# A flow-matching backbone step on one core: two projection chunks per norm tile, and another order of the PSUM pairs

## The chip, the cores and the metric

One core of a Trainium2 chip runs the kernel. The metric is device time in microseconds (us), the median of several executions. The engines are PE (TensorE, matmuls), ACT (ScalarE), DVE (VectorE), POOL (GpSimd) and SP (SyncE, which here only issues the weight DMAs). They run side by side and wait for each other through semaphores only.

## The reference, cut to what matters

The model has two layers. Each one norms its 640 tokens (128 context, 512 latent) and multiplies them with one wide input matrix; everything else in the layer hangs on that product.

```python
D_MODEL = 1024; DEPTH = 2; SEQ = 128; DEC_SEQ = 512
...
def trunk_layer(x, cond, p, rope, ctx_k, ctx_v):
    mod = (jax.nn.silu(cond) @ p['mod_w'] + p['mod_b']).reshape(-1, 1, 6 * D)
    sh1, sc1, g1, sh2, sc2, g2 = jnp.split(mod, 6, axis=-1)
    h = rms_norm(x, p['norm1_w']) * (1 + sc1) + sh1
    proj = h @ p['w_in']
    hy, qkv, scv, gates = jnp.split(proj, [HY_COLS, HY_COLS + ATT_COLS, HY_COLS + ATT_COLS + SC_COLS], axis=-1)
    ya = hyena_mixer(hy, ...)     # starts with a 3-tap convolution over the tokens
    ...                           # attention, short convolution, gates, merge, experts
```

## The kernel before, in words

**Layout.** Activations lie feature-major: `X` is 128 partitions x 8 tiles of features (KC = 8) x 640 tokens. Weights come as a stream of 1 MB items into the four slots of `ring`; SP issues the load of an item when `item_used` says that the last user of its slot is done (L419).

**Precision.** A product of fp32 operands is made of three fast passes. Weights and activations are each split into a high and a low part, and high x high, high x low and low x high are added (`passes`). ACT copies the high part of a half item (128 output features) to `W2` (`split`, L1008), DVE subtracts it to get the low part (L1348). `W2` has two places, so the split of half item u waits for the end of the chunk that used u - 2.

**A chunk** (`chunk`, L557) is 128 output features for all tokens: 8 feature tiles x 3 passes x 2 halves of 320 tokens = 48 matmuls of 128x320, each with its own weight load, accumulated in a pair of PSUM banks. The pairs are numbered 0 (banks 0, 1), 1 (banks 2, 3) and 2 (banks 4, 5); chunk c of the first 24 uses pair c % 3. Its last matmul raises `chunk_ready`. Banks 6 and 7 take transposes.

**The norm** at the head of a layer. PE makes the mean squares (L570), ACT the root (L1034), DVE the reciprocal, and PE spreads it over the partitions into pair 1 (L575). Then, feature tile by feature tile, DVE multiplies X by it (L1371, in two pieces: 128 and 512 tokens), ACT adds the shift and rounds to the high part (L1039), and DVE makes the low part (L1360) and raises `x_lo`, once a tile. DVE runs one tile ahead: L1371 of tile k + 1, then L1360 of tile k.

**The first chunks.** PE's loop over c = 0 to 23 is written out in program order: wait for the split half item c (`half_ready`, which for odd c also raises `item_used`), for c of 3 or more wait for the pair to be free, then the chunk; behind chunks 1 to 8 come the transposes of the chunk before it (`transposes(c - 1)`, L682, five of 128x128). Chunk 0 alone waits for `x_lo` before each feature tile. Chunk 1 runs after it without waits inside.

**What a chunk sets off.** For c below 12, ACT waits for chunk c, copies it from PSUM to `raw` in two pieces (L1008, 128x128 and 128x512), then splits half item c + 2. DVE splits half item c + 2 too and then makes the 3-tap convolution of `raw` into `cv` (`conv`: L1508 and two times L1511, 128x641), and raises `conv_done`. `transposes(c)` waits for that. All queues are in order.

Of the kernel before, what the change touches and what calls it, by code (L numbers as in the profile page):

```python
# [28 lines left out]
KC = D // P  # L29
DEPTH = 2  # L30
LI, LS = 128, 512
T = LI + LS
# [3 lines left out]
HALVES = ((0, T // 2), (T // 2, T))  # L36
# [66 lines left out]
def build(nc, a):  # L103
    with ExitStack() as ctx:
# [43 lines left out]
        ps = ctx.enter_context(nc.psum_tensor("ps", [P, 8, 512], F32))  # L148
# [36 lines left out]
        Y3 = region(56, [3, 4, T])  # L185
        u_tm, x1_tm = region(86, [NT, DH]), region(96, [NT, DH])
        qkv = region(106, [NT, QKV])
        raw, cv = region(121, [2, T + 3]), region(126.25, [2, T + 1])
        ubuf = region(131.5, [2, T])
# [61 lines left out]
        x_hi, x_lo = sem("operand_hi"), sem("operand_lo")  # L251
        OP_Y, OP_M, OP = KC, KC + 12, KC + 12 + KC
        w_hi, w_lo = sem("weights_hi"), sem("weights_lo")
        chunk_ready = sem("chunk_ready")
        act_freed, dve_freed = sem("act_freed"), sem("dve_freed")
# [68 lines left out]
        def tokh(b):  # L324

            return ps[:, 2 * b:2 * b + 2, :].rearrange("p a n -> p (a n)")[:, 192:832]

        def w2(u, kc, part):

            return W2[:, u % 2, part, :].rearrange("p (k n) -> p k n", k=kc)  # L330
# [208 lines left out]
        def _(pe):  # L539
# [11 lines left out]
            def chunk(b, w, src, n, wait=None):  # L551

                for k, wp, hp, first, last in passes(n):
                    if wait and wp + hp == 0:
                        wait(k)
                    for c0, c1 in HALVES:
                        mm = pe.matmul(tokh(b)[:, c0:c1], w(wp)[:, k, :], src(hp, k)[:, c0:c1], start=first, stop=last)  # L557
                return mm
# [109 lines left out]
            for l in range(DEPTH):  # L668
# [13 lines left out]
                        mm = pe.transpose(ps[:, 6 + t // 4, P * (t % 4):P * (t % 4) + P], cv[:, c % 2, cols], ident[:])  # L682
                    mm.then_inc(tr_ready, 1)

                for c in range(24):
                    half_ready(l, c)
                    if c >= 3:
                        wait_chunk_freed(pe, l, c - 3)

                    wait = (lambda k: pe.wait_ge(x_lo, l * OP + k + 1)) if c == 0 else None  # L690
                    chunk(c % 3, lambda part: w2(c, KC, part), h_part, KC, wait).then_inc(chunk_ready, 1)
                    if 1 <= c <= 8:
                        transposes(c - 1)
                for i in range(3):

                    for hf in range(2):
                        half_ready(l, 24 + 2 * i + hf)
                        for u in range(3):
                            n = 24 + 3 * i + u
                            if hf == 0:  # L700
                                wait_chunk_freed(pe, l, n - 3)
                            for t in range(2 * u, min(2 * u + 2, NT)):
                                for k, wp, hp, first, last in passes(4):
                                    mm = pe.matmul(ps[:, 2 * (n % 3) + t % 2, 0:256],  # L704
                                                   h_part(hp, 4 * hf + k)[:, P * t:P * t + P],
                                                   w2(hf, 4, wp)[:, k, :], start=first and hf == 0, stop=last and hf == 1)
                            if hf or u == 2:
                                mm.then_inc(chunk_ready, 1)
# [15 lines left out]
                for t in range(NT):  # L724
                    if t >= 2:
                        pe.wait_ge(a_trev, l * 6 + t - 1)
                    for j in range(4):
                        mm = pe.transpose(ps[:, t % 2, P * j:P * j + P], qkv[:, t, P * j:P * j + P], ident[:])
                    mm.then_inc(a_tr, 1)
                for t in range(NT):  # L730
                    mm = pe.transpose(ps[:, 2 + (t + 3) // 4, P * ((t + 3) % 4):P * ((t + 3) % 4) + P],
                                      qkv[:, t, NQ * HD:QK], ident[:])
# [48 lines left out]
                for j in range(4):  # L781
                    for g in range(2):
                        mm = pe.matmul(ps[:, 4 + g, P * j:P * j + P], qT[head(g), j, 0:P], kT[head(g), 0:P],
                                       start=True, stop=True)
# [3 lines left out]
                for g in range(2):  # L788
                    for j in range(4):
                        mm = pe.transpose(ps[:, 4 + g, P * j:P * j + P], Pp[:, g, P * j:P * j + P], ident[:])  # L790
# [3 lines left out]
                for g in range(2):  # L794
                    mm = pe.matmul(ps[head(g), 6, :], qkv[:, 0, QK + HD * g:QK + HD * g + HD], PTp[:, g, :],
                                   start=True, stop=True)
# [13 lines left out]
                for o in range(2):  # L810
# [35 lines left out]
                    for r in range(2):  # L846
                        mm = pe.matmul(ps[:, 4 + r, :], csi[:, r, :], u_tm[:, 0, :], start=True, stop=True)
# [4 lines left out]
                    if o == 0:  # L852
                        for r in range(2):
                            mm = pe.matmul(ps[:, 6, :], csi[:, r, :], Yp[:, r, :], start=r == 0, stop=r == 1)
                    else:
                        for m in range(4):
                            for r in range(2):
                                mm = pe.matmul(ps[:, 6, P * m:P * m + P], Yp[:, r, P * m:P * m + P], csi[:, r, :],
                                               start=r == 0, stop=r == 1)
# [35 lines left out]
                for n in range(2 * NT):  # L895
                    t, hf = n // 2, n % 2
# [109 lines left out]
        def _(act):  # L1006
            def copy(o, i):
                return act.activation(o, i, ACT.Copy)  # L1008
# [101 lines left out]
            for l in range(DEPTH):  # L1110
# [13 lines left out]
                for c in range(24):  # L1124
                    if 2 <= c <= 9:
                        evac_tr(c - 2)
                    if freed_by(c)[0] == "act":
                        wait_chunk(act, l, c)
                        if c < 12:
                            if c >= 2:  # L1130

                                act.wait_ge(conv_done, l * 12 + c - 1)
                            copy(raw[:, c % 2, 1:1 + LI], tokh(c % 3)[:, 0:LI])
                            copy(raw[:, c % 2, 2 + LI:2 + T], tokh(c % 3)[:, LI:T]).then_inc(act_freed, 1)
                        else:
                            if c >= 18:
                                act.wait_ge(dve_freed, l * 8 + c % 2 + 1)
                            copy(ubuf[:, c % 2, :], tokh(c % 3)).then_inc(act_freed, 1)
                    split(l, c + 2)
                for n in range(9):  # L1140
                    i, u = n // 3, n % 3
                    if u == 0:

                        split(l, 26 + 2 * i)
                    wait_chunk(act, l, 24 + n)
                    t1 = min(2 * u + 2, NT)
                    b = 2 * ((24 + n) % 3)
                    copy(qkv[:, 2 * u:t1, 256 * i:256 * i + 256], ps[:, b:b + t1 - 2 * u, 0:256]).then_inc(act_freed, 1)
                    if u == 2:
                        split(l, 27 + 2 * i)  # L1150
# [190 lines left out]
        def _(dve):  # L1341
# [152 lines left out]
            for l in range(DEPTH):  # L1494
# [20 lines left out]
                for c in range(24):  # L1515
                    b = c % 2
                    settle()
                    split(l, c + 2)
                    if c < 12:
                        before = (c // 2) * 2 + c % 2  # L1520
                        dve.wait_ge(act_freed, l * A_FREED + before + 1)
                        if 2 <= c < 8 or c in (8, 9):
                            dve.wait_ge(tr_ready, l * 8 + c - 1)
                        ins = conv(cv[:, b, :], lambda i: raw[:, b, i:i + T + 1], V_HYW + 3 * c, V_HYB + c)
                        if c < 8:
                            ins.then_inc(conv_done, 1)
                        else:
                            settle()
                            dve.tensor_copy(Y3[:, 0, c - 8, 0:LI], cv[:, b, 0:LI])
                            dve.tensor_copy(Y3[:, 0, c - 8, LI:T], cv[:, b, LI + 1:T + 1]).then_inc(conv_done, 1)  # L1530
                        continue
                    if freed_by(c)[0] == "act":
                        continue
                    j = 2 * ((c - 12) // 6) + b
                    settle()
                    wait_chunk(dve, l, c)
                    pieces = ((0, LI, 0), (LI, T, 1))
                    if (c - 12) % 6 < 4:

                        dve.wait_ge(act_freed, l * A_FREED + freed_by(12 + 6 * ((c - 12) // 6) + b)[1])  # L1540
                        for c0, c1, x in pieces:
                            ins = dve.tensor_tensor(raw[:, b, 1 + c0 + x:1 + c1 + x], tokh(c % 3)[:, c0:c1],
                                                    ubuf[:, b, c0:c1], ALU.mult)
                        ins.then_inc(dve_freed, 1)
                        settle()
                        conv(cv[:, b, :], lambda i: raw[:, b, i:i + T + 1], V_SCW + 3 * j, V_SCB + j)
                    else:
                        for c0, c1, x in pieces:
                            ins = dve.tensor_tensor(Y3[:, 2, j, c0:c1], tokh(c % 3)[:, c0:c1],
                                                    cv[:, b, c0 + x:c1 + x], ALU.mult)  # L1550
                        ins.then_inc(dve_freed, 1)

# [404 lines left out]
```

## Time and profile before

| | |
|---|---|
| Median of 3 runs | 2566.1 us (2566.07 to 2567.58) |
| The profiled execution | 2564.07 us |
| Its span | 2562.4 us |
| PE busy | 2286.4 us (89%) |
| DVE, ACT, POOL busy | 1122.7, 739.0, 162.5 us |
| Granted PE clock, mean of the span | 0.938 |
| PE's share of the chain that ended last | 82% |

The profile is of one execution. The chain that ended last is followed back from the last instruction, at each step to what released it; an engine's share of it tells how much of the end hangs on that engine. The granted clock is a share of PE's full speed: 1.0 is 2.4 GHz, 0.5 is 1.2 GHz. Layer 0 begins at about 260 us of the span and layer 1 at about 1410 us; before layer 0 lies a prologue.

### The profile page before, as it was taken

The page shows a single profiled execution, that of the slowest core. Times are in us where ns is not written, and L with a number is a line of the kernel's source. Part 1 is how long each engine was busy: PE and PEld are TensorE (multiplying, and loading weights), DVE is VectorE, ACT ScalarE, POOL GpSimd, SP SyncE. Part 2 cuts the span into 40 slices and gives each one's busy share as a digit, 9 for nine tenths or more (in the row PEclk, how much of TensorE's full clock was granted, in tenths as well). Part 3 has the DMA queues.
Part 4 walks back from the last instruction along what each step waited for, and adds up shares of the span by engine and source line. Part 5 has one row for each costly group of instructions (what it writes and reads, how often), then busy time and mean ns, then how long its engine had stood idle before and what let it go on. Part 6 is the DMA issues. An engine that isn't in the chain of part 4 may idle for free.

```text
span 2562.4 us, 35187 instructions
## 1 busy us (share of the span) xinstructions
PE 2286.4 (89%) x13744; PEld 1840.1 (72%) x13744; DVE 1122.7 (44%) x1778; ACT 739.0 (29%) x1302; POOL 162.5 (6%) x218
## 2 busy tenths in 40 slices
PE   4999899999797998599996899999787998699995
PEld 2444799999663996466664899999654996466664
DVE  2454544341358654333334544331368654333333
ACT  1332321222350223133332321222350323233332
POOL 0001000000100100011110000000100100011100
PEclk8599899999998998799998899999898998799998
DMA  8687112133401431899993122233401421899992
GB/s 304 230 317 282 64 67 83 72 132 113 172 1 41 141 114 60 296 350 346 344 341 119 56 77 72 77 128 123 161 1 41 155 101 75 292 355 345 341 330 93
DMA packets 71938, 436.28 MB, mean 170 GB/s; under 512 B 9225, under 2 KB 9737, under 8 KB 30794
## 3 DMA queue, kind: packets, MB, share of 16 engines
q1 hardware_dynamic: 45216, 329.27, 35.3%
q0 software_dynamic: 21872, 89.44, 11.4%
q10 hardware_dynamic: 4732, 15.93, 1.7%
q8 instruction: 82, 1.34, 0.2%
q14 instruction: 36, 0.29, 0.0%
HBM read 384.46 MB, written 50.15 MB: 170 GB/s over the span
## 4 chain that ended last, share of the span: by engine, by line
PE 82%; DVE 7%; DMA 4%; ACT 3%; issue 2%; DVEq 1%; ACTq 0%; POOLq 0%; POOL 0%
PE ps L557 36%; PE ps L939 17%; PE ps L962 7%; PE ps L704 3%; PE ps L639 2%; PE ps L591 2%; PE ps L621 2%; DMA back<-in_cft 1%; PE ps L747 1%; PE ps L836 1%; PE ps L833 1%; PE ps L599 1%; PE ps L819 1%; PE ps L892 1%; ACT front L1008 1%
## 5 line engine op out<-in xcount | busy, mean ns | idle before, releaser
L557 PE MATMUL ps<-front_r 128*128 128x320 f32 x5888 | 935.0, 312 | 25.0 <-DVE front_r L1360 10.4
L557 PEld LDWEIGHTS ps<-front_r 128*128 128x128 f32 x5888 | 886.3, 190 | 31.4 <-issue 10.3
L1348 DVE TENSOR_TENSOR front_r<-ring,front_r 128x1024 fp32r<-128x1024 f32 x148 | 181.0, 1224 | 465.8 <-ACT front_r L1008 464.7
L1008 ACT ACTIVATE front_r<-ring 128x1024 fp32r<-128x1024 f32 x148 | 156.0, 1055 | 395.7 <-PE ps L557 292.9
L1008 ACT ACTIVATE back<-ps 128x480 f32<-128x480 f32 (+4 forms) x236 | 111.3, 496 | 438.3 <-PE ps L557 165.9
L939 PE MATMUL ps<-ring,back 128*80 128x256 f32 x1024 | 231.5, 386 | 1.9 <-ACT back L1008 1.9
L939 PEld LDWEIGHTS ps<-ring,back 128*80 128x80 f32 x1024 | 154.9, 153 | 70.4 <-issue 6.6
L962 PE MATMUL ps<-back_r,front_r 128*80 128x512 f32 x768 | 198.8, 404 | 0.0
L939 PE MATMUL ps<-front,back 128*80 128x256 f32 x768 | 168.3, 379 | 0.0
L939 PEld LDWEIGHTS ps<-front,back 128*80 128x80 f32 x768 | 115.1, 150 | 51.0
L557 PE MATMUL ps<-back_r,front_r 128*128 128x320 f32 x640 | 148.4, 314 | 0.0
L962 PEld LDWEIGHTS ps<-back_r,front_r 128*80 128x80 f32 x768 | 109.0, 148 | 52.0
L1775 DVE TENSOR_TENSOR back<-ps,back 80x256 f32<-80x256 f32 x64 | 26.9, 421 | 260.7 <-PE ps L939 260.7
L557 PEld LDWEIGHTS ps<-back_r,front_r 128*128 128x128 f32 x640 | 109.4, 192 | 0.0
L1292 ACT ACTIVATE back<-ps 80x256 f32<-80x256 f32 x64 | 24.3, 379 | 294.4 <-PE ps L939 294.4
L1158 ACT ACTIVATE back<-ps 128x640 f32<-128x640 f32 x48 | 33.8, 705 | 229.1 <-PE ps L557 229.1
L1008 ACT ACTIVATE front<-ps 128x512 f32<-128x512 f32 (+3 forms) x126 | 62.7, 564 | 113.6 <-PE ps L819 83.2
L591 PE MATMUL ps<-ring,cs 128*32 128x256 f32 x768 | 67.8, 483 | 22.4 <-ACT back L1008 11.3
L704 PE MATMUL ps<-front_r 128*128 128x256 f32 x720 | 86.7, 283 | 0.0
L704 PEld LDWEIGHTS ps<-front_r 128*128 128x128 f32 x720 | 86.6, 192 | 0.0
L528 POOL DMA_INDIRECT acc<-back,idx x32 | 45.8, 1432 | 595.9 <-issue 559.5
L1787 DVE TENSOR_TENSOR back_r<-front,back_r 128x512 fp32r<-128x512 f32 x128 | 81.1, 684 | 3.2 <-ACT back_r L1008 3.1
(208 smaller groups left out, 2431.3 us busy)
## 6 DMA issues: line engine op xcount, KB each, us to landing
ring<-in_stream SPq DMA_DIRECT2D x186, 1024.0 KB, 5.9
front<-in_stream SPq DMA_DIRECT2D x80, 1024.0 KB, 8.6
back<-in_stream SPq DMA_DIRECT2D x48, 1024.0 KB, 7.5
gates<-back POOLq DMA_DIRECT2D x48, 320.0 KB, 2.4
back<-gates POOLq DMA_DIRECT2D x48, 320.0 KB, 3.3
kspec<-back POOLq DMA_DIRECT2D x20, 512.0 KB, 6.7
back<-kspec POOLq DMA_DIRECT2D x4, 2560.0 KB, 11.9
rows<-front ACTq DMA_DIRECT2D x10, 520.0 KB, 2.7
```

The costliest lines, as they stand in the source:

```text
L528: pool.indirect_dma_start(a[f"acc{l}"], bass.IndirectOffsetOnAxis(ap=idx[:, e:e + 1], axis=0), yo[:, e % 2, :], None, compute_op=ALU.add). ...
L557: mm = pe.matmul(tokh(b)[:, c0:c1], w(wp)[:, k, :], src(hp, k)[:, c0:c1], start=first, stop=last)
L591: mm = pe.matmul(ps[32 * j:32 * j + 32, 6, 0:256], cs[:, k, :], w[:, k, :], start=k < 4, stop=k >= 4)
L621: mm = pe.matmul(ps[:, 4 + d, :], fh2[l][:, P * t:P * t + P], w3[:, l, w0:w0 + DH], start=True, stop=True)
L639: mm = pe.matmul(ps[:, b + odd, :], cft[:, r, 2 * odd + t, P * kt:P * kt + P], (fa, fb)[r][:, unit % 2, 1 + 2 * odd + t, :], start=t == 0, ...
L704: mm = pe.matmul(ps[:, 2 * (n % 3) + t % 2, 0:256], h_part(hp, 4 * hf + k)[:, P * t:P * t + P], w2(hf, 4, wp)[:, k, :], start=first and hf ...
L939: mm = pe.matmul(ps[0:SLOTS, 2 * hf + which, 0:256], x[:, k, :], w[:, k, :], start=k == 0, stop=k == KC - 1)
L962: mm = pe.matmul(ps[0:SLOTS, 6 + c, :], hidT[hp][:, ee % 2, k, :], W4[:, v % 4, wp, :], start=k + n == 0, stop=k == 3 and n == 2)
L1008: return act.activation(o, i, ACT.Copy)
L1158: act.activation(sgb[:, n % 2, :], tokh(n % 4), ACT.Sigmoid).then_inc(sg_ready, 1)
L1348: dve.tensor_tensor(half_dst(u, 1), src, half_dst(u, 0).bitcast(F32), ALU.subtract).then_inc(w_lo, 1)
L1787: dve.tensor_tensor(W4[:, v % 4, 1, :], quarter_item(l, ee, v)[1], W4[:, v % 4, 0, :].bitcast(F32), ALU.subtract).then_inc(e_wlo, 1)
```

## The change

The first two chunks of each layer are worked together. PE waits for both half items at the start, then for each feature tile of the norm it issues the six matmuls of chunk 0 and the six of chunk 1, pass by pass in turn. `chunk_ready` is raised by chunk 0's last matmul and by chunk 1's. The loop goes on with `transposes(0)` and chunk 2. The pairs of banks are used in the order 0, 2, 1, since pair 1 holds the spread root until the norm's last tile; every place that names a pair for the first 33 chunks goes through `third`.

```diff
+        def third(c):
+            return (0, 2, 1)[c % 3]
...
+                half_ready(l, 0)
+                half_ready(l, 1)
+                for k, wp, hp, first, last in passes(KC):
+                    if wp + hp == 0:
+                        pe.wait_ge(x_lo, l * OP + k + 1)
+                    for c in range(2):
+                        for c0, c1 in HALVES:
+                            mm = pe.matmul(tokh(third(c))[:, c0:c1], w2(c, KC, wp)[:, k, :], h_part(hp, k)[:, c0:c1],
+                                           start=first, stop=last)
+                        if last:
+                            mm.then_inc(chunk_ready, 1)
-                for c in range(24):
+                for c in range(1, 24):
+                    if c == 1:
+                        transposes(0)
+                        continue
                     half_ready(l, c)
                     if c >= 3:
                         wait_chunk_freed(pe, l, c - 3)
-                    wait = (lambda k: pe.wait_ge(x_lo, l * OP + k + 1)) if c == 0 else None
-                    chunk(c % 3, lambda part: w2(c, KC, part), h_part, KC, wait).then_inc(chunk_ready, 1)
+                    chunk(third(c), lambda part: w2(c, KC, part), h_part, KC).then_inc(chunk_ready, 1)
                     if 1 <= c <= 8:
                         transposes(c - 1)
```

The readers of the pairs on ACT and DVE change `c % 3` to `third(c)` in the same way, and nothing else; these two engines, POOL and SP issue the same instructions in the same order as before.

PE's order around the head of layer 0, of the kernel before, from the norm's sixth tile to chunk 3 (`front_r` holds the split weights and activations, `operand_lo` is the semaphore `x_lo`, `weights_lo` is `w_lo`; line 557 is `chunk`, line 682 the transposes):

```order
L557 MATMUL ps<-front_r 128x320 [waits operand_lo]
L557 MATMUL ps<-front_r 128x320 x5
L557 MATMUL ps<-front_r 128x320 [waits operand_lo]
L557 MATMUL ps<-front_r 128x320 x5
L557 MATMUL ps<-front_r 128x320 [waits weights_lo]
L557 MATMUL ps<-front_r 128x320 x47
L682 MATMUL ps<-ident,back 128x128 [waits conv_done]
L682 MATMUL ps<-ident,back 128x128 x4
L557 MATMUL ps<-front_r 128x320 [waits weights_lo]
L557 MATMUL ps<-front_r 128x320 x47
```

The same place of PE in the changed kernel (line 697 is the new loop, 561 is `chunk`, 686 the transposes):

```order
L697 MATMUL ps<-front_r 128x320 [waits operand_lo]
L697 MATMUL ps<-front_r 128x320 x11
L697 MATMUL ps<-front_r 128x320 [waits operand_lo]
L697 MATMUL ps<-front_r 128x320 x11
L686 MATMUL ps<-ident,back 128x128 [waits conv_done]
L686 MATMUL ps<-ident,back 128x128 x4
L561 MATMUL ps<-front_r 128x320 [waits weights_lo]
L561 MATMUL ps<-front_r 128x320 x47
```

The 48 matmuls that stood between the last feature tile and the transposes of chunk 0 now stand ahead of that tile's end, six with each of the eight tiles; the transposes, with their wait on `conv_done`, follow the norm's last tile directly.

## Rows read from the trace of the kernel before

**Rows 1.** The page: engines over the span, and the chain that ended last

```profile
PE 2286.4 (89%) x13744; PEld 1840.1 (72%) x13744; DVE 1122.7 (44%) x1778; ACT 739.0 (29%) x1302; POOL 162.5 (6%) x218
PE 82%; DVE 7%; DMA 4%; ACT 3%; issue 2%; DVEq 1%; ACTq 0%; POOLq 0%; POOL 0%
```

**Rows 2.** The chain, head of layer 0: start us, us, what

```profile
267.87 1.02 DVE front L1371 x2
...
281.10 0.94 DVE front_r L1360 x2
...
282.07 1.14 PE ps L557 x6
...
283.25 8.19 PE ps L557 x54
291.43 0.59 PE ps L682 x5
292.02 7.04 PE ps L557 x48
```

**Rows 3.** The chain, head of layer 1

```profile
1432.50 8.18 PE ps L557 x54
```

**Rows 4.** Timeline of layer 0: start us, us, engine line op, tiles, count [idle before <-releaser]

```profile
271.12 6.58 PE L557 MATMUL ps<-front_r 128*128 128x320 f32 x24 [3.29 <-DVE front_r L1360]
272.87 1.57 PEld L557 LDWEIGHTS ps<-front_r 128*128 128x128 f32 x6 [0.21 <-DVE front_r L1360]
...
283.24 7.92 PEld L557 LDWEIGHTS ps<-front_r 128*128 128x128 f32 x54 [0.29 <-DVE front_r L1360]
283.34 29.34 SPq L419 DMA_DIRECT2D ring<-in_stream  x3
284.49 0.77 ACT L1008 ACTIVATE back<-ps 128x128 f32<-128x128 f32 x2 [2.35 <-PE ps L557]
...
286.23 1.23 DVE L1348 TENSOR_TENSOR front_r<-ring,front_r 128x1024 fp32r<-128x1024 f32 x1 [3.04 <-ACT front_r L1008]
...
288.06 1.85 DVE L1511 SCALAR_TENSOR_TENSOR back<-back,vec 128x641 f32<-128x641 f32 x2
```

**Rows 5.** Windows: busy of PE, PEld, DVE, ACT, POOL, then granted clock, DMA, GB/s

```profile
270.00:276.00 6.00, 4.88 (x17) 4.43 (x18) 6.00 (x14) 3.27 (x8) 0.00 (x0) 0.50 0.01 3
276.00:277.00 1.00, 0.99 (x6) 0.73 (x6) 1.00 (x3) 0.62 (x2) 0.00 (x0) 0.88 0.00 0
1426.00:1427.00 1.00, 1.00 (x6) 1.00 (x6) 1.00 (x4) 0.30 (x1) 0.00 (x0) 0.73 0.00 0
684.00:686.00 2.00, 0.00 (x0) 0.00 (x0) 1.85 (x3) 0.63 (x2) 0.00 (x0) 0.96 1.04 422
686.00:689.00 3.00, 2.79 (x10) 2.08 (x12) 1.41 (x5) 0.78 (x1) 0.00 (x0) 0.50 1.02 418
689.00:690.00 1.00, 1.00 (x10) 0.51 (x8) 0.00 (x0) 0.24 (x1) 0.00 (x0) 0.87 1.04 426
675.00:676.00 1.00, 1.00 (x6) 0.64 (x5) 0.00 (x0) 0.65 (x2) 1.00 (x2) 0.70 0.13 33
935.00:938.00 3.00, 3.00 (x14) 3.00 (x13) 2.79 (x4) 0.30 (x1) 0.00 (x0) 0.50 0.00 0
938.00:940.00 2.00, 2.00 (x14) 2.00 (x13) 0.00 (x0) 0.00 (x0) 0.00 (x0) 0.89 0.00 0
```

**Rows 6.** Timeline of PE: restarts after idle stretches, and 128x320 matmuls at either clock

```profile
672.53 4.23 PE L728 MATMUL ps<-ident,back 128*128 128x128 f32 x20 [7.72 <-POOLq L294]
686.21 1.97 PE L790 MATMUL ps<-ident,front 128*128 128x128 f32 x8 [5.71 <-DVE front L1637]
933.58 0.56 PE L557 MATMUL ps<-front_r 128*128 128x320 f32 x2 [1.89 <-DVE back L1712]
935.24 1.27 PE L557 MATMUL ps<-front_r 128*128 128x320 f32 x4
936.31 0.73 PE L557 MATMUL ps<-back_r,front_r 128*128 128x320 f32 x2
```

More of the change, by code:

```diff
@@ L703, in _ @@
                                 for k, wp, hp, first, last in passes(4):
-                                    mm = pe.matmul(ps[:, 2 * (n % 3) + t % 2, 0:256],
+                                    mm = pe.matmul(ps[:, 2 * third(n) + t % 2, 0:256],
                                                    h_part(hp, 4 * hf + k)[:, P * t:P * t + P],
@@ L1132, in _ @@
                                 act.wait_ge(conv_done, l * 12 + c - 1)
-                            copy(raw[:, c % 2, 1:1 + LI], tokh(c % 3)[:, 0:LI])
-                            copy(raw[:, c % 2, 2 + LI:2 + T], tokh(c % 3)[:, LI:T]).then_inc(act_freed, 1)
+                            copy(raw[:, c % 2, 1:1 + LI], tokh(third(c))[:, 0:LI])
+                            copy(raw[:, c % 2, 2 + LI:2 + T], tokh(third(c))[:, LI:T]).then_inc(act_freed, 1)
                         else:
@@ L1137, in _ @@
                                 act.wait_ge(dve_freed, l * 8 + c % 2 + 1)
-                            copy(ubuf[:, c % 2, :], tokh(c % 3)).then_inc(act_freed, 1)
+                            copy(ubuf[:, c % 2, :], tokh(third(c))).then_inc(act_freed, 1)
                     split(l, c + 2)
@@ L1146, in _ @@
                     t1 = min(2 * u + 2, NT)
-                    b = 2 * ((24 + n) % 3)
+                    b = 2 * third(24 + n)
                     copy(qkv[:, 2 * u:t1, 256 * i:256 * i + 256], ps[:, b:b + t1 - 2 * u, 0:256]).then_inc(act_freed, 1)
@@ L1541, in _ @@
                         for c0, c1, x in pieces:
-                            ins = dve.tensor_tensor(raw[:, b, 1 + c0 + x:1 + c1 + x], tokh(c % 3)[:, c0:c1],
+                            ins = dve.tensor_tensor(raw[:, b, 1 + c0 + x:1 + c1 + x], tokh(third(c))[:, c0:c1],
                                                     ubuf[:, b, c0:c1], ALU.mult)
@@ L1548, in _ @@
                         for c0, c1, x in pieces:
-                            ins = dve.tensor_tensor(Y3[:, 2, j, c0:c1], tokh(c % 3)[:, c0:c1],
+                            ins = dve.tensor_tensor(Y3[:, 2, j, c0:c1], tokh(third(c))[:, c0:c1],
                                                     cv[:, b, c0 + x:c1 + x], ALU.mult)
```

## The prediction

> **What bounds the kernel now.** I read the page first: PE is busy for 89% of the span and carries 82% of the chain that ended last [rows 1]. So a stage is worth what it adds to or takes from PE's path. The chain then shows the place of the change [rows 2]. From 267.87 to 282.03 us it runs through DVE alone: L1371 and L1360 in turn, 0.92 to 1.02 us each, so a feature tile comes about every 1.84 us: PE takes up the second at 272.87 and the seventh at 282.07 [rows 2, 4]. PE waits for each. From 283.25 the chain is PE without a break: the last tile of chunk 0 (6 matmuls) and chunk 1 (48) in 8.19 us, the transposes in 0.59, chunk 2 in 7.04, which is 0.147 us a matmul. Layer 1 has the same step, 54 matmuls in 8.18 us [rows 3]. The reader should see that chunk 1 does two jobs: it fills PE, and it covers the way from chunk 0's end to the convolution that `transposes(0)` waits for.
>
> I count from S, the start of PE's first matmul on a tile: 271.12 [rows 4]. Chunk 2 starts at 292.02, so at S + 20.90, in layer 0. That is the figure to beat.
>
> **What the change takes away.** Chunk 1's own 7.04 us behind the norm are gone, in each layer. The number of matmuls and weight loads is the same.
>
> **What the joint tiles take.** In the first tiles PE has the 1.2 GHz clock. It shows 0.50 in 270 to 276 and 0.88 in 276 to 277, so it rises at 276.24, 5.1 us after S; in layer 1 0.73 in 1426 to 1427 puts the rise at 1426.54, 6.2 us after that layer's first tile at 1420.4 (1432.50 less the 12.1 us from 271.12 to 283.25) [rows 3 to 5]. At that clock four matmuls of 128x320 take 1.07 us (935.24 to 936.31), 0.267 each [rows 6]. Six take 1.6 us, which just fits a tile's 1.84; twelve take 3.2 and do not. So PE falls behind DVE as long as the clock is low. At the full clock twelve take 1.76 us, no more than a tile's cadence, so PE doesn't catch up either: the joint stretch is bound by PE, not DVE. With a low stretch of x us it ends at S + x + (96 - x / 0.267) x 0.147. For x I take 4.2 us, the mean of the time spent working at the low clock at five restarts that I can read: 5.1 and 6.2 here, 3.1 from 672.53 (the 0.70 in 675 to 676 puts the rise at 675.6), 3.1 from 686.21 (the 0.87 in 689 to 690 puts it at 689.3) and 3.4 from 935.0, behind the restart at 933.58 (0.89 in 938 to 940: 938.4) [rows 5, 6]. That gives 16 matmuls at 0.267 and 80 at 0.147: **the joint stretch ends at S + 16.0** (15.5 with 3.1 us, 16.9 with 6.2). Before, chunk 1 ended at 291.43, S + 20.3. So 4.3 us are won, not 7.04.
>
> **What the change adds: a wait.** `transposes(0)` now follows at once and waits for `conv_done`. The way to it hangs on chunk 0's end, which now lies two matmuls before the joint end. Before, chunk 0's last matmul started at about 283.98 (the sixth at 0.147 from 283.24) and ACT took up the copy at 284.49, 0.51 later. The convolution ended at 288.06 + 1.85 = 289.91 [rows 4]. So 5.42 us lie between ACT's start and its end: two copies, ACT's split, DVE's split of 1.23 and three convolution steps, all in series, with both engines idle before them (2.35 and 3.04 us). None of it starts sooner now. Chunk 0's last matmul starts 0.44 before the joint end, so ACT starts 0.07 after it, and the transposes can start at 0.07 + 5.42 + 0.05 (DVE's end to PE's start, as the 0.03 from 281.10 + 0.94 to 282.07 [rows 2]) = **5.54 us after the joint end**. In that time PE has nothing: chunk 2 stands behind the transposes, though its weights are split 3.0 us after the joint end (287.46 against 284.49). Before, the convolution was done 1.5 us before PE came to it, so the cover was there, with little to spare.
>
> **What the wait does to the clock.** An idle stretch of 5.71 us before 686.21 left the clock at 0.96 in 684 to 686 and at 0.50 from 686 on; even one of 1.89 us before 933.58 was followed by a low stretch, 935 to 938.4 [rows 5, 6]. So after 5.5 us idle I take the low clock for granted. Work went on at it for 3.1 to 6.2 us in the five cases above, 4.2 in the mean, and half of that is lost: **2.1 us** (1.55 to 3.1). The transposes are in it (20 take 4.23 us at the low clock [rows 6], so five take 1.06 in place of 0.59). They matter in one more way. In [rows 5] the clock rose at 675.6 while the engine had done nothing but the transposes of L728. I go by that: the five transposes count as work from their first. The Trainium skill, in TensorE: Matmul & The Clock Gate, Part 4 on the PE-mode transpose, says that the full clock does not engage for transposes, as they do not count as busy in the same way. By that rule the return would be counted only from chunk 2, 1.06 us later, which costs 0.5 us more in each layer and makes the total below 2573.8; the trace speaks against it.
>
> **Sum for a layer.** 16.0 + 5.54 + 0.59 (transposes) + 2.1 = S + 24.2, against S + 20.9: **3.3 us later**. From chunk 2 on the cadence is as before: chunk 3 needs the split that DVE makes right behind the first convolution, 1.23 us, and transposes(1) its convolution 2.5 us later, both within chunk 2's 7.04. The delay is not absorbed, since PE carries the chain to the layer's end.
>
> **Costed at nothing.** The order of the banks: the same number of PSUM accesses, and the halves of one chunk already alternate between two banks at 0.147 us. Waiting for both half items at the start: both are split before the root is spread. The load of a weight item: `item_used` for the first item is raised some 18 us sooner, so SP's DMA moves from 283.34 [rows 4] to the norm; at its old place DVE's split beside it took 1.23 us, as long as later ones, and PE waits for no load in this stage.
>
> **Total.** Two layers: +6.7 us (twice 3.33). On the profiled execution's own 2564.07 us that is 2570.8; its time lies 2.0 us under the median, so against the median of 2566.1 it gives **2572.8 us**. About 0.2%, 5.1 us, is what a measurement of this kernel can tell from no change.
>
> **Rivals.**
> *The clock holds through the wait.* Then 2.1 us a layer fall away and a layer loses 16.0 + 5.54 + 0.59 - 20.9 = 1.2 us, 2.5 in all: 2568.6 us, no measurable change. Against it stand 684 to 689 and 935 to 938 in [rows 5]; for it only that a drop may come late.
> *Not slower: PE keeps pace with the norm.* If the denser work brought the clock up with the first tile, the joint stretch would be bound by DVE. It would end 12 matmuls after the last tile, which came at 283.24 (S + 12.1): S + 13.9. With the clock also held, chunk 2 starts at S + 20.0, 0.9 us sooner, 1.8 us in all: 2564.3 us. It decides from a joint stretch of under 14.8 us. Against it: in layer 1 the clock rose only 6.2 us after S [rows 5], though six matmuls a tile keep PE at work 1.6 us of 1.84 at that clock.
> *Interleaving four banks slows the matmuls,* or a chunk behind waits as well. At 0.02 us a matmul it is 2 us a layer more: 2576.7 us. Nothing in the trace shows such a price.
> *The change doesn't do what it says:* if DVE's tiles slowed beside twice the matmuls, the stretch would be bound by DVE after all; since PE sets it with 2 us to spare, this costs nothing until a tile takes over 2.1 us.
>
> **How the numbers follow.** My forecast has 0.83, of it 0.75 slower by over 5.1 us and 0.08 under that, since its bounds are 15.5 + 5.54 + 0.59 + 1.55 - 20.9 = 2.3 us and 16.9 + 5.54 + 0.59 + 3.1 - 20.9 = 5.2 us a layer, 4.6 and 10.4 in all. The clock that holds has 0.07, the pace kept 0.05 (0.02 of it in a gain over 0.2%, from what I don't see), slower matmuls 0.05. That makes 0.80 slower, 0.18 the same, 0.02 faster. The range takes in the held clock below (2568.6) and the upper bound (2576.5): 2568.5 to 2577.
>
> **What would show it.** In the changed profile: joint matmuls without a gap from the second tile on, ending about 16 us after the first; then PE idle for 5.5 us, released by DVE's L1511 step (its convolution) in both layers; then a granted clock of 0.5 for some 3 to 6 us; chunk 2 starting 3 us later than now, counted from the first tile. I am wrong if that idle stretch is under 4 us, if the clock stays at 1.0 behind it, or if the joint stretch ends before S + 15.

## The result, and the profile after

The changed kernel takes 2574.38 us (median of 8 runs, 2572.67 to 2575.86) against 2566.8 us before (8 runs, 2566.07 to 2567.86). The ratio is 1.0028 with a 95% interval of 1.0017 to 1.0039: slower by 7.6 us in the medians, 4.4 to 10.0 by the interval. The forecast was 2572.8 us, slower. It was added up on the median of 2566.1 us that stood on record for the kernel before; its own difference was 6.7 us, against the 7.6 measured.

The engines' busy times are nearly as before (PE 2288.7 us against 2286.4 in [rows 1]). The time went where PE has nothing to do, and into the clock behind it. Below is the chain of waits of the changed kernel at the head of layer 0, to be laid beside [rows 2]. Each line has its start in us, its length in us, and what ran. Line 697 is the joint loop, 561 `chunk`, 686 the transposes, 1026 ACT's copies, 1366 DVE's split, 1378 DVE's low part of an activation tile, 1529 the convolution:

```profile
272.18 1.02 DVE front_r L1378 x2
273.21 0.04 issue
273.25 16.78 PE ps L697 x94
...
290.12 0.07 ACT back L1026
...
290.77 1.07 ACT front_r L1026
291.83 0.02 issue
291.86 1.23 DVE front_r L1366
...
294.64 0.90 DVE back L1529
295.55 0.04 issue
295.59 1.33 PE ps L686 x5
296.92 8.39 PE ps L561 x48
305.30 0.59 PE ps L686 x5
305.89 7.04 PE ps L561 x48
```

Three things are to be seen. The steps of DVE for seven more tiles, which [rows 2] had, are gone: the chain is on PE from the first tile on, 94 matmuls without a gap (the 94th is chunk 0's last). Then it leaves PE for ACT and DVE, at 290.03, and comes back at 295.59; before, it never left PE there. And the first transposes and chunk 2 are longer, 1.33 and 8.39 us in place of 0.59 and 7.04. Layer 1 shows the same, with a longer chunk 2:

```profile
1426.46 15.46 PE ps L697 x94
...
1447.47 1.33 PE ps L686 x5
1448.80 9.19 PE ps L561 x48
1457.99 0.59 PE ps L686 x5
```

The timeline names in brackets how long the engine was idle before a line, and what released it; first two lines of layer 0, then one of layer 1:

```profile
273.25 17.06 PE L697 MATMUL ps<-front_r 128*128 128x320 f32 x96 [3.19 <-DVE front_r L1378]
295.59 1.33 PE L686 MATMUL ps<-ident,back 128*128 128x128 f32 x5 [5.28 <-DVE back L1529]
1447.47 1.33 PE L686 MATMUL ps<-ident,back 128*128 128x128 f32 x5 [5.28 <-DVE back L1529]
```

And the windows, with the columns of [rows 5], give the granted clock, third from the end:

```profile
279.00:280.00 1.00, 1.00 (x7) 1.00 (x7) 1.00 (x3) 0.33 (x2) 0.00 (x0) 0.85 0.00 0
280.00:292.00 12.00, 10.31 (x71) 10.05 (x69) 5.41 (x12) 4.61 (x11) 0.00 (x0) 1.00 0.01 1
292.00:293.00 1.00, 0.00 (x0) 0.00 (x0) 1.00 (x2) 1.00 (x2) 0.00 (x0) 0.97 0.00 0
293.00:299.00 6.00, 3.41 (x14) 3.41 (x15) 5.61 (x8) 1.12 (x2) 0.00 (x0) 0.50 0.00 0
299.00:300.00 1.00, 1.00 (x6) 1.00 (x5) 0.30 (x1) 0.00 (x0) 0.00 (x0) 0.61 0.00 0
1429.00:1430.00 1.00, 1.00 (x6) 1.00 (x6) 1.00 (x3) 0.80 (x2) 0.00 (x0) 0.71 0.00 0
1446.00:1447.00 1.00, 0.00 (x0) 0.00 (x0) 0.93 (x2) 0.00 (x0) 0.00 (x0) 0.82 0.00 0
1453.00:1454.00 1.00, 1.00 (x7) 1.00 (x6) 0.00 (x0) 0.00 (x0) 0.00 (x0) 0.76 0.00 0
```

A window's mean clock between 0.5 and 1.0 tells when it changed: 0.85 over one microsecond is 0.3 us at half speed and 0.7 us at full speed. So the 2.4 GHz level came at 279.3, went at 292.9 in the middle of the idle stretch, and was back at 299.8, 4.2 us after PE took up work. In layer 1 it came at 1429.6, went at 1446.6 and was back at 1453.5, 6.0 us after PE's restart at 1447.47.

Counted from PE's first matmul on a tile, chunk 2 ended 305.30 - 273.25 = 32.05 us later in layer 0 and 31.53 in layer 1; before it was 299.06 - 271.12 = 27.94 in both (chunk 2's end is 292.02 + 7.04 in [rows 2]). That is +4.11 and +3.59, 7.7 us together, which agrees with the measured loss of 7.6. The two spans differ by 10.6 us; 2.1 of the other 2.9 lie ahead of layer 0 (first tile at 273.25 against 271.12), where both kernels have the same instructions. Across all profiles of this study that first tile lay anywhere between 271.0 and 273.25, so it is no part of the change.

### The profile page after: what moved, and what is told of

It reads as the page before. It is cut to its first block, busy times and chain, and to the rows that moved or that the text cites. A ratio compares the mean times of both kernels' runs of the same rounds, so it can differ in the third digit from the quotient of the medians.

```text
span 2573.0 us, 35185 instructions
## 1 busy us (share of the span) xinstructions
PE 2288.7 (89%) x13744; PEld 1844.1 (72%) x13744; DVE 1123.0 (44%) x1778; ACT 739.0 (29%) x1302; POOL 162.8 (6%) x218
## 4 chain that ended last, share of the span: by engine, by line
PE 82%; DVE 7%; DMA 4%; ACT 3%; issue 2%; DVEq 1%; ACTq 0%; POOLq 0%; POOL 0%
PE ps L561 35%; PE ps L957 17%; PE ps L980 7%; PE ps L722 3%; PE ps L595 2%; PE ps L643 2%; PE ps L625 2%; DMA back<-in_cft 1%; PE ps L765 1%; PE ps L697 1%; PE ps L854 1%; PE ps L851 1%; PE ps L837 1%; PE ps L603 1%; PE ps L910 1%
## 5 line engine op out<-in xcount | busy, mean ns | idle before, releaser
L561 PE MATMUL ps<-front_r 128*128 128x320 f32 x5696 | 902.1, 311 | 14.6 <-DVE back_r L1710 8.2
L561 PEld LDWEIGHTS ps<-front_r 128*128 128x128 f32 x5696 | 857.5, 190 | 16.8 <-DVE front_r L1366 8.9
L1026 ACT ACTIVATE front_r<-ring 128x1024 fp32r<-128x1024 f32 x148 | 156.0, 1055 | 395.9 <-PE ps L561 292.9
L722 PEld LDWEIGHTS ps<-front_r 128*128 128x128 f32 x720 | 86.6, 192 | 0.0
```

The source lines that it names most:

```text
L722: mm = pe.matmul(ps[:, 2 * third(n) + t % 2, 0:256], h_part(hp, 4 * hf + k)[:, P * t:P * t + P], w2(hf, 4, wp)[:, k, :], start=first and h ...
```

## The experiments

Theory A is the forecast's: the loss is PE's wait for the first convolution, plus the low clock behind it. Theory B puts it on the PSUM side: other banks, or more of them in turn, make the matmuls dearer. Each run stands beside runs of the kernel before on the same chip, whose medians were 2566.38 (runs 1, 2, 4, 5), 2566.27 (runs 3, 7, 8, 9) and 2565.83 us (runs 6, 10). The ratios are against these. Where a run is set against the changed kernel's 2574.38, that one stood beside a kernel before of 2566.8; counted from the kernel before on either side, such a gain is 0.4 to 1.0 us smaller.

**1. The order of the banks alone.**

```diff
-                half_ready(l, 0)
-                half_ready(l, 1)
-                for k, wp, hp, first, last in passes(KC):
...
-                for c in range(1, 24):
-                    if c == 1:
-                        transposes(0)
-                        continue
+                for c in range(24):
...
-                    chunk(third(c), lambda part: w2(c, KC, part), h_part, KC).then_inc(chunk_ready, 1)
+                    wait = (lambda k: pe.wait_ge(x_lo, l * OP + k + 1)) if c == 0 else None
+                    chunk(third(c), lambda part: w2(c, KC, part), h_part, KC, wait).then_inc(chunk_ready, 1)
```

> Only the order of the PSUM pairs (0, 2, 1) is taken from the change; chunks 0 and 1 run one after the other as before. Theory A (the loss is the wait of the transposes on the first convolution, plus the low clock behind it): no difference from before, 2566.8 us within 1 us, and chunk 2 starts 20.9 us after PE's first matmul on a tile. Theory B (other banks or more of them in turn make PE's accesses dearer): part of the 7.6 us shows here, at least 2 us.

Measured: 2566.0 us, ratio 1.0 (0.9991 to 1.0009). Its chain has the steps of [rows 2] to a hundredth:

```profile
284.01 8.18 PE ps L561 x54
292.19 0.59 PE ps L686 x5
292.77 7.04 PE ps L561 x48
```

The order of the banks is free, within the 2.3 us to either side that the interval leaves, and by the chain to a hundredth. It is what permits the joint chunks, not what they cost.

**2. A shorter wait: the split of half item 2 in place of the convolution.** On the changed kernel:

```diff
-                for c in range(1, 24):
-                    if c == 1:
-                        transposes(0)
-                        continue
+                for c in range(2, 24):
...
-                    if 1 <= c <= 8:
-                        transposes(c - 1)
+                    if 2 <= c <= 9:
+                        transposes(c - 2)
```

> The changed kernel with every group of transposes one chunk later: chunk 2 comes straight behind the joint chunks, then the transposes of chunk 0, chunk 3, the transposes of chunk 1 and so on. Theory A: PE now waits only for DVE's split of half item 2, 3.0 us after the joint end in place of 5.5, so 2.5 us a layer are won back; the clock still falls, a little less often. 5 to 6 us less than the changed kernel's 2574.4, so 2568 to 2569.5 us. Theory B: nothing is won by it, 2574 us.

Measured: 2567.55 us, ratio 1.0003 (0.9994 to 1.0012); 6.8 us less than the changed kernel, half a microsecond under what was expected. The timeline:

```profile
290.95 8.62 PE L561 MATMUL ps<-front_r 128*128 128x320 f32 x48 [2.83 <-DVE front_r L1363]
1439.19 8.83 PE L561 MATMUL ps<-front_r 128*128 128x320 f32 x48 [2.83 <-DVE front_r L1363]
```

PE now waits 2.83 us for line 1363, DVE's split, and 48 matmuls still take 8.62 and 8.83 us where the timeline has 7.3 for them at the full clock. So 2.45 us of wait are gone in each layer; the clock costs 1.3 and 1.5 in place of 2.1 and 2.9.

**3. The control: the later transposes on the kernel before.** The same last two lines, on the kernel before.

> The kernel before with every group of transposes one chunk later and nothing else. Theory A: before the change no wait of PE stood there, so the later transposes win nothing by themselves: 2566.4 us within 1 us. If the later transposes were a gain of their own, under 2564 us, what the second run won would not be the shorter wait.

Measured: 2566.07 us, ratio 0.9998 (0.9989 to 1.0007). The later transposes gain nothing where nobody waits for them; what run 2 won is the shorter wait, and the shorter low clock behind it.

**4. The wait filled with idle matmuls.** On the changed kernel, behind the joint loop:

```diff
+                for n in range(34):
+                    c0, c1 = HALVES[n % 2]
+                    pe.matmul(tokh(1)[:, c0:c1], h_hi[:, 0, 0:P], h_hi[:, 0, 0:T // 2], start=True, stop=True)
```

> The changed kernel with 34 idle matmuls of 128x320 behind the joint chunks (operands from the high activations, output to pair 1, which chunk 2 overwrites), 5.0 us of work in a wait of 5.5. Theory A: chunk 2 starts at the same place, but the granted clock stays at 1.0 through the wait and the 2.1 us (layer 0) and 2.9 us (layer 1) that the transposes and chunk 2 lost at the low clock are back: 2574.4 - 5.0 = 2569.4 us. If the clock had no part in it: 2574.4 us or more.

Measured: 2567.61 us, ratio 1.0006 (0.9997 to 1.0015). The chain of layer 0:

```profile
272.47 16.08 PE ps L697 x94
...
294.12 0.81 PE ps L686 x5
294.92 7.04 PE ps L561 x48
```

The window over the wait:

```profile
288.00:296.00 8.00, 7.70 (x54) 7.44 (x53) 5.30 (x7) 4.02 (x7) 0.00 (x0) 1.00 0.00 0
```

The transposes still wait for the convolution (294.12, which is 21.65 us after the first tile, within what the changed kernel's two layers show: 22.34 and 21.01). But the clock stays at 1.00 and chunk 2 takes 7.04. In this profile chunk 2 ends 29.49 us after the first tile, 1.55 more than before; in layer 1 it is 1.1 more. That is the forecast's rival of the held clock, 1.2 us a layer, made real. The run won 6.8 us, or 6.4 counted from the kernel before on either side, where 5.0 were expected; the difference lies within the interval, whose half width is 2.3 us. The clock's part of the loss is thereby shown by itself: by the trace 5.0 of 7.7 us, with 2.65 left.

**5. More cover: chunk 1 three tiles behind chunk 0.**

```diff
+                def tile(c, k):
+                    if c == 0:
+                        pe.wait_ge(x_lo, l * OP + k + 1)
+                    for wp, hp in ((0, 0), (0, 1), (1, 0)):
...
+                for k in range(KC + 3):
+                    if k < KC:
+                        tile(0, k)
+                    if k >= 3:
+                        tile(1, k - 3)
```

> Chunk 1 works three feature tiles behind chunk 0 in place of beside it, so chunk 0 takes the last tile as soon as it is there and four tiles of chunk 1, 24 matmuls or 3.5 us, are left to cover the way to the first convolution. Transposes stay where the change has them. Theory A: chunk 0 ends about 13.0 us after PE's first tile, chunk 1 at 16.5, the convolution at 18.8: PE waits 2.3 us in place of 5.5, and chunk 2 starts 19.4 us plus a clock loss of 0 to 2 us after the first tile, against 20.9 before and 22.2 plus 2.5 in the changed kernel: 2563 to 2567 us. Theory B (the alternation between two chunks costs): no better than 2573 us.

Measured: 2566.73 us, ratio 1.0002 (0.9993 to 1.0011): 7.6 us less than the changed kernel, but at the upper end of what was expected.

```profile
291.84 1.33 PE L686 MATMUL ps<-ident,back 128*128 128x128 f32 x5 [2.06 <-DVE back L1534]
1441.05 0.80 PE L686 MATMUL ps<-ident,back 128*128 128x128 f32 x5 [2.06 <-DVE back L1534]
```

Those are lines of the timeline. The chain of layer 0 goes on:

```profile
291.84 1.33 PE ps L686 x5
293.17 8.04 PE ps L561 x48
```

The wait is 2.06 us, 2.3 had been worked out, but everything lies 0.7 us later: tile 7 of chunk 0 still stands behind the matmuls of chunk 1 that precede it. And even these two microseconds brought the low clock: 1.33 and 8.04 us in place of 0.59 and 7.04, so 1.7 us a layer. In layer 1 the chain has 0.80 and 8.58, 1.75 us too much, though the clock went down only 1.1 us behind the restart. Cover that is a little too short costs the wait once and the clock as well.

**6. Still more cover: six tiles behind.** `KC + 6`, `k >= 6` and `k - 6` in the loop of run 5.

> Chunk 1 six tiles behind chunk 0, the transposes where the change has them: the cover behind chunk 0's end goes from 2 matmuls (the change) past 24 (three tiles behind) to 36, 5.3 us. Theory A: chunk 0 ends 13.1 us after the first tile, chunk 1 at 18.4, the convolution is done at 18.9. PE waits about 0.5 us, the clock holds, and chunk 2 starts at 19.5 against 20.9 before: 1.4 us a layer, 2563.6 us. If a clock loss or another wait stays: 2566 us or more.

Measured: 2566.18 us, ratio 1.0001 (0.9992 to 1.001).

```profile
283.08 9.06 PE ps L697 x60
292.14 0.59 PE ps L686 x5
292.73 7.04 PE ps L561 x48
```

No wait and no low clock, as expected, but the gain of 1.4 us a layer was a slip of mine: behind chunk 0's end seven tiles of chunk 1 are left, 42 matmuls, not 36, which is 0.9 us; and ACT took up chunk 0's copy 14.06 us after the first tile, where 13.1 had been expected for chunk 0's end. Chunk 2 starts 292.73 - 272.02 = 20.7 us after the first tile, against 20.9. With so much kept for cover, nearly all of chunk 1 is behind the norm again. Runs 5 and 6 show both ends. Four or five tiles behind were not run. In run 6 the convolution ended at 291.50, 0.64 us before the transposes started, so an estimate is that less cover could win at most 0.6 us a layer more: what covers the 5.4 us to the convolution is the same work that the change wanted to move ahead.

**7. Cover and a shorter wait together.** Run 5's loop with run 2's transposes.

> Chunk 1 three tiles behind chunk 0, and the transposes one chunk later. Theory A: in the run with chunk 1 behind alone, the joint work ended 17.2 us after the first tile and DVE's split of half item 2 at about 17.0, so PE finds no wait at all and the clock stays up. Chunk 3 starts at 17.2 + 7.04 + 0.59 = 24.8 us after the first tile, against 28.3 before: 3.5 us a layer, 2559.5 us. If the split comes late by over a microsecond or the clock falls all the same: 2562 to 2564 us.

Measured: 2560.44 us, ratio 0.9977 (0.9967 to 0.9987), faster than both kernels. The chain:

```profile
276.52 11.95 PE ps L697 x78
288.47 7.04 PE ps L561 x48
295.51 0.58 PE ps L686 x5
296.10 7.04 PE ps L561 x48
```

PE goes from the joint chunks into chunk 2 without a gap and at the full clock. Chunk 3 starts 296.10 - 271.00 = 25.1 us after the first tile, against 299.65 - 271.12 = 28.5 before, 3.4 us less; in layer 1 it is 3.3. But only one group of transposes stands ahead of it here, and two stood there before, so 0.59 us of this is put off and not saved. The two kernels are level again behind chunk 9. First the kernel before, then this run:

```profile
344.82 0.59 PE ps L682 x5
```

```profile
341.86 7.04 PE ps L561 x48
348.90 0.59 PE ps L686 x5
```

Before, chunk 9 started behind these transposes, at 345.41, and took 7.04, so chunk 10 started 352.45 - 271.12 = 81.3 us after the first tile. Here chunk 9 starts at 341.86 and the transposes stand behind it; chunk 10 starts 349.49 - 271.00 = 78.5 us after the first tile, 2.8 us sooner; in layer 1 it is 2.7. The sum is 5.6, measured were 5.8. The expected 3.5 us a layer left out the same 0.59.

**8. The low clock ahead of the first tile.** On the changed kernel:

```diff
+                for n in range(12):
+                    c0, c1 = HALVES[n % 2]
+                    pe.matmul(tokh(2)[:, c0:c1], w2(0, KC, 0)[:, 0, :], W2[:, 0, 0, 0:T // 2], start=True, stop=True)
```

> The changed kernel with the same 12 idle matmuls ahead of the first tile. Theory A: the joint stretch, which PE bounds, is shorter by 0.45 of the low time that is saved, about 1.4 us a layer, and ends at or above 13.9 us after the first tile; the wait of 5.5 us and the low clock behind it stay: 2574.4 - 2.8 = 2571.6 us. If DVE's tiles bound the joint stretch: 2574.4 us.

Measured: 2569.55 us, ratio 1.001 (1.0001 to 1.0019), 4.8 us less than the changed kernel where 2.8 were expected.

```profile
272.86 14.84 PE L700 MATMUL ps<-front_r 128*128 128x320 f32 x96 [0.24 <-DVE front_r L1381]
292.98 1.33 PE L686 MATMUL ps<-ident,back 128*128 128x128 f32 x5 [5.28 <-DVE back L1532]
```

The joint stretch takes 14.84 us in place of 17.06 and 15.74, and the wait of 5.28 us is what it was. So the joint stretch is bound by PE, and its excess is the low clock. That is 3.1 us in both layers together, near the 2.8 expected. By the chain chunk 2 took 7.90 us in layer 0 and 8.10 in layer 1, in place of 8.39 and 9.19: the low clock behind the wait was also shorter in this execution, which is the other 1.6 us and nothing that the edit was meant to do. At the full clock the joint stretch ends 14.7 us after the first tile, not 13.9 as the forecast's rival had it: tile 6, the seventh, is there only at S + 10.95, and from it on 24 matmuls are to be done, 3.5 us.

**9. The same 12 idle matmuls on run 7.**

> As the run before it, with 12 idle matmuls of 128x320 between the spread of the root and the first tile, where PE waits for 3.2 us (output to pair 2, which chunk 1 overwrites). Theory A: the clock comes up about 3 us sooner, PE is less far behind when the last tile comes and the joint work ends up to 1.4 us a layer sooner: 2557 us, 2559.5 if chunk 0 was bound by DVE's tiles alone.

Measured: 2559.13 us, ratio 0.9972 (0.9961 to 0.9983), the lowest median of all, but within the interval of run 7's. Its chain has 11.96 and then 7.04 us, as run 7's; chunk 3 starts 296.74 - 271.63 = 25.1 us after the first tile, no sooner. With chunk 1 three tiles behind, PE is not late in the first tiles, so a faster clock there only lengthens its waits. By its size the outcome is the second of the two expected.

**10. The weight item given free as late as before.** On the changed kernel:

```diff
-                half_ready(l, 1)
+                pe.wait_ge(w_lo, l * UNITS + 2)
...
+                pe.sem_inc(item_used, 1)
```

> The changed kernel with one part undone: the first weight item is given free behind the joint chunks, as late as before the change, so SP's load does not fall into the norm. Theory A costs this part at nothing: 2574.4 us within 1 us. Rival: the load beside the norm slows something, and at least 1.5 us are won.

Measured: 2572.89 us, ratio 1.0026 (1.0017 to 1.0036) against the change's 1.0028. SP's load is issued behind the norm again, at 285.40 us, 13.8 us after the first tile; in the changed kernel it was at 267.70, 5.6 us ahead of it. The wait has not changed:

```profile
293.38 1.33 PE L686 MATMUL ps<-ident,back 128*128 128x128 f32 x5 [5.28 <-DVE back L1530]
```

The median is 1.5 us lower, but the kernel before was 1.0 us lower beside it; counted from that one the loss is 7.1 us in place of 7.6, and the load costs nothing that can be told.

## Why the prediction was right

**The joint stretch is bound by PE and ends at S + 16.0: right.** The records end at S + 17.06 and S + 15.74; a record runs on for 0.16 us past its matmul's turn of 0.147 (0.31 in all), so the stretch ended at S + 16.9 in layer 0 and S + 15.6 in layer 1. The spread follows the clock as the formula has it: a low stretch of 6.05 us (273.25 to 279.3) gives 16.8, one of 3.1 (1426.46 to 1429.6) gives 15.5. Run 8 is the same formula with the low stretch taken away. The forecast's 4.2 us for the low stretch was right in neither layer; 16.0 lies between the two ends, and that their mean, 16.25, comes so near it is in part luck.

**The wait: right to a tenth.** Forecast were 5.54 us from the joint end; the transposes started at 22.34 and 21.01 us, so 5.4 after it in both layers. ACT took up the copy at 290.12 and the transposes started at 295.59, 5.47 us, of which the forecast had 5.42 and 0.05. Runs 2, 5 and 6 change the wait's end or its cover, and it goes to 2.83, 2.06 and nothing.

**The clock behind it: right in kind, a little small.** 2.1 us a layer was the estimate, from restarts elsewhere in the trace. It measured (1.33 - 0.59) + (8.39 - 7.04) = 2.1 in layer 0 and 0.74 + 2.15 = 2.9 in layer 1. The forecast's reckoning that half of the low time is lost held: 2.1 us of 4.2, and 2.9 of 6.0. Against the forecast's 3.3 us a layer, layer 0 lost 0.8 more, all of it in the joint stretch (+0.9, with -0.1 from the wait); layer 1 lost 0.3 more (-0.4 in the joint stretch, -0.1 in the wait, +0.8 in the clock). Run 4 shows the clock's part by taking it away. The clock was back 4.2 and 6.0 us after the first transpose, within the 3.1 to 6.2 of the five restarts. The five transposes took 1.33 us, 0.267 each, where the forecast had 1.06: it took the mean of the 20 from 672.53, of which the last ones already ran at the full clock ([rows 5], from 675.6). The rule in the Trainium skill's TensorE: Matmul & The Clock Gate, Part 4 on the PE-mode transpose, that the full clock does not engage for transposes, could not be told from this here, as 1.33 us of them stand ahead of 8 us of matmuls; [rows 5, 6], where it rose beside transposes alone, stay the evidence against it, in the trace of before.

**What was costed at nothing.** The order of the banks (run 1), the earlier load (run 10) and the cadence from chunk 2 on (7.04 and 0.59 in the chain above) cost nothing that the runs can tell. That four banks in turn are free too follows from run 8: 96 joint matmuls in 14.7 us, where the tiles' arrival alone asks for 14.5.

**The rivals.** The held clock happened only in run 4, where it was held by work. The pace kept happened only in run 8; its bound of S + 13.9 was 0.6 us too low, since it left out that tile 6 comes only 1.17 us ahead of the last. DVE's tiles did not slow beside twice the matmuls: in layer 0 its line 1378 starts at 274.03, 275.87, 277.71 and 279.55, 1.84 us apart as before. One slip in the reading of [rows 2] changes nothing: the chain from 267.87 to 282.03 is not DVE alone, 1.02 us of it, at 268.91, are ACT's (L1039).

## What to carry to other kernels

When work is moved ahead of a wait, look first at what it covered where it stood: chunk 1 hid a chain of ACT and DVE of 5.4 us. Moving its 7.0 us ahead won only 3.4 and 4.7 us (the joint end against S + 20.3), because PE itself bound the joint stretch, and the uncovered wait and the clock behind it cost more than that. Work of two streams pass by pass makes both end at the same time, and so late; let the stream whose end sets something off lead, with enough of the other left behind it, and let the next work in the queue be what is ready first (run 7: 5.8 us under the kernel before, while each half alone, runs 2 and 5, only gave back the loss). A wait of PE is dearer than its length: here 5.4 us idle cost 2.1 to 2.9 more.

## What was not expected of the hardware

A wait of 2.06 us between dense matmuls brought the low clock as well (run 5, 1.7 us lost in each layer), as one of 1.89 us had done in [rows 6]; but the pauses of 0.7 us ahead of the last three tiles of the kernel before did not. And the same code has its low stretches at other places from layer to layer: 6.05 and 3.1 us at the norm, 4.2 and 6.0 behind the wait, in one execution. An estimate from these: 1.3 us between the two joint ends and 0.8 us between the two chunks 2, so about 2 us by which an execution of the changed kernel can move; its eight executions lie 3.2 us apart.
